# Attention steps taken in pairs, with the inserted projection tiles spread over the pairs, in a hybrid gMLP and differential-attention layer

## What is computed

```
h = rms_norm(x) * (1 + scale(c)) + shift(c)
u_a, v_a, z_a, q, k, v, z_b = split(h @ w_in)            # seven blocks of 512 columns
a_out = u_a * (tril(w_s) @ rms_norm(v_a) + b_s) * silu(z_a)       # chunks of 128 positions
q, k = rope(rms_norm(q)), rope(rms_norm(k))              # 8 half heads of 64
for each of 4 heads, causal:
    o = (softmax(q1 k1^T / 8) - lam * softmax(q2 k2^T / 8)) @ v     # v: 128 wide
b_out = rms_norm(o) * (1 - lam_init) * silu(z_b)
x = x + gate(c) * (concat(a_out, b_out) @ w_out)
```

## Time and profile before

| | |
|---|---|
| time, median of 3 runs | 527.22 us (526.07, 529.1, 527.22) |
| the profiled execution's own time | 524.75 us |
| its span, slowest core (core 0) | 523.7 us |
| spans of the eight cores | 518.9 to 523.7 us |
| mean granted TensorE clock by core | 0.969 to 0.977 |
| TensorE busy | 443.3 us (85% of the span) |
| VectorE busy | 334.4 us (64%) |
| ScalarE busy | 299.6 us (57%) |
| attention loop | about 273 to 489 us |
| after the last step | 489 to 523.7 us |

### The profile page before, as it was taken

How to read it: one execution, slowest core, us unless ns; L and a number is a source line. 1 busy time by engine, 2 the same in 40 slices (tenths; PEclk the granted TensorE clock), 3 DMA queues, 4 the chain that set the end, 5 groups by cost and what they waited for, 6 DMA issues and landing times.

```text
span 523.7 us, 9735 instructions; the slowest of 8 cores (518.9 to 523.7 us)
## 1 busy us (share of the span) xinstructions
PE 443.3 (85%) x3104; PEld 213.6 (41%) x3104; DVE 334.4 (64%) x761; ACT 299.6 (57%) x402; POOL 85.0 (16%) x118
## 2 busy tenths in 40 slices
PE   0036697999999999999979999989997999999395
PEld 0002243444444443443326554444554555555242
DVE  1236845664765478888872676788658857868732
ACT  1056477446543247677777666666777778777100
POOL 1112500003760000000001111122222222122100
PEclk9998989999999999999988999999999999999979
DMA  8998989237433200050021212116822032011113
GB/s 200 269 304 233 253 295 132 65 58 164 102 139 103 81 1 2 1 76 6 1 80 41 63 61 77 46 42 206 279 83 82 27 98 80 13 70 41 41 69 133
DMA packets 15605, 53.90 MB, mean 103 GB/s; under 512 B 2242, under 2 KB 2626, under 8 KB 14660
## 3 DMA queue, kind: packets, MB, share of 16 engines
q1 hardware_dynamic: 13924, 45.36, 26.8%
q0 software_dynamic: 1152, 7.50, 9.1%
q10 hardware_dynamic: 480, 0.41, 0.3%
HBM read 50.29 MB, written 8.39 MB: 112 GB/s over the span
## 4 chain that ended last, share of the span: by engine, by line
PE 62%; DMA 10%; DVE 8%; ACT 7%; issue 6%; POOL 4%; SPq 0%; DVEq 0%; ACTq 0%; POOLq 0%
PE psum L648 14%; PE psum L470 13%; PE psum L1045 9%; PE psum L923 8%; DMA sb_WO<-w_adaT 5%; PE psum L893 5%; PE psum L1011 4%; ACT sb_cs L906 4%; DMA sb_kT<-xT 4%; POOL sb_cs L911 4%; PE psum L682 2%; DVE sb_F L980 2%; PE psum L669 1%; DVE sb_F L939 1%; PE psum L671 1%
## 5 line engine op out<-in xcount | busy, mean ns | idle before, releaser
L906 ACT ACTIVATE sb_cs<-psum,sb_small 128x1024 bf16<-128x1024 f32 x144 | 151.0, 1114 | 58.6 <-PE psum L893 58.6
L923 PE MATMUL psum<-sb_vB,sb_cs 128*128 128x129 bf16 x1088 | 88.2, 223 | 9.6 <-POOL sb_cs L911 6.1
L923 PEld LDWEIGHTS psum<-sb_vB,sb_cs 128*128 128x128 bf16 x1088 | 63.3, 99 | 39.8 <-issue 39.3
L911 POOL TENSOR_TENSOR sb_cs<-sb_cs,sb_constb 128x256 bf16<-128x256 bf16 x64 | 44.3, 695 | 216.4 <-ACT sb_cs L906 211.9
L470 PE MATMUL psum<-sb_W,sb_hT 128*128 128x512 bf16 x256 | 62.3, 404 | 15.5 <-ACT sb_hT L466 12.6
L893 PE MATMUL psum<-sb_qT,sb_kT 64*128 64x256 bf16 (+1 forms) x576 | 56.4, 272 | 6.5 <-ACT sb_cs L906 2.9
L648 PE MATMUL psum<-sb_hT,sb_W 128*128 128x512 bf16 x256 | 60.2, 378 | 0.0
L357 DVE SCALAR_TENSOR_TENSOR sb_F<-sb_WO,sb_F 128x1024 f32<-128x1024 f32 x24 | 30.2, 1258 | 30.5 <-DMA sb_WO<-w_adaT 22.0
L470 PEld LDWEIGHTS psum<-sb_W,sb_hT 128*128 128x128 bf16 x256 | 25.8, 102 | 51.5 <-issue 26.1
L436 PE MATMUL psum<-sb_vnA,sb_constb 128*128 128x512 bf16 x32 | 11.0, 471 | 32.5 <-ACT sb_vnA L429 32.5
L939 DVE COPY sb_F<-psum 128x258 f32<-128x258 f32 x64 | 24.2, 420 | 20.4 <-PE psum L923 20.3
(11 more groups left out here) (113 smaller groups left out, 543.2 us busy)
## 6 DMA issues: line engine op xcount, KB each, us to landing
sb_WO<-w_adaT SPq DMA_DIRECT2D x24, 512.0 KB, 7.6
sb_W<-w_in POOLq DMA_DIRECT2D x5, 1024.0 KB, 10.5
sb_W<-x SPq DMA_DIRECT2D x8, 512.0 KB, 4.9
sb_cs<-w_out SPq DMA_DIRECT2D x8, 512.0 KB, 3.5
sb_hT<-x SPq DMA_DIRECT2D x8, 512.0 KB, 12.2
out<-sb_hT SPq DMA_DIRECT2D x8, 512.0 KB, 2.8
out<-sb_W SPq DMA_DIRECT2D x6, 512.0 KB, 3.2
sb_qT<-xT SPq DMA_DIRECT2D x4, 512.0 KB, 22.7
```

Of the source, the lines that this page charges most:

```text
L906: act(lambda E: E.activation(out=et, in_=psum[:, X:X + 2, :], func=AF.Exp, bias=negM, scale=0.125), reads=[pb[X], pb[Y], b_lam], writes=[b ...
L911: pool(lambda E, em=em: E.tensor_tensor(out=em, in0=em, in1=tri_b.unsqueeze(1).broadcast_to([128, 2, 128]), op=ALU.mult), reads=[b_e[ei], ...
L923: pe(lambda E, u=u, j=j, c=c, i=i: E.matmul(psum[:, j, 256 * c:256 * c + 129], lhsT=et[:, c, QB * u + 128 * j:QB * u + 128 * (j + 1)], rhs ...
```

## The change

The loop over steps becomes a loop over 72 pairs of steps. A pair issues exp of both steps, QK of the next two, then 4 or 5 matmuls of inserted tiles in turn (`quota`), PV of the first step, PV of the second. If the first of the two steps ends a group, its PV and `group_end` stand ahead of the inserted matmuls, which then lie between the two PV. A tile may be cut across pairs; it is evacuated at the end of the pair in which it was finished. Transposes are not counted in the quota. Per pair one or two tasks are popped. Eight matmuls, those of the two gate tiles, are issued ahead of the first pair. After the loop, tiles may use banks 2 to 7. All tasks and the last `fin_head` are issued, then up to 40 matmuls of output tiles, and only then the transposes of the last block. The functions that make tiles return their matmuls as a list, with the evacuation, in place of issuing them; `uu_owner` is an assertion and issues nothing.

```diff
-            later(now[0] + (2 if now[0] < NS else 0), outs)
-        return post
+            if h1 == 4:
+                later(now[0] + (2 if now[0] < NS else 0), outs)
+        return [mm], post
...
-    FB = [2, 3]
+    FB = [[2, 3]]
...
-    def fill_one():
-        it = fillq.pop(0)
-        kind, run, wt = it[0:3]
-        bank = FB[fb_ctr[0] % 2]
+    def open_tile():
+        it = fillq.pop(0)
+        kind, run = it[0:2]
+        bank = FB[0][fb_ctr[0] % len(FB[0])]
         fb_ctr[0] += 1
-        posts.append(run(bank))
...
+        if any(b_ == bank for b_, _ in posts):
+            run_posts()
+        mms, post = run(bank)
+        cur.append((kind, mms, bank, post))
+
+    def fill(n):
+        while n > 0 and (cur or fillq):
+            if not cur:
+                open_tile()
+            kind, mms, bank, post = cur[0]
+            if kind == "tr":
+                n += 1
+            while mms and n > 0:
+                mms.pop(0)()
+                n -= 1
+            if not mms:
+                cur.pop()
+                posts.append((bank, post))
...
-    ets = {}
-    for gs in range(NS + 1):
-        now[0] = gs
-        if gs < NS:
-            ets[gs] = do_exp(gs)
-        if gs + 2 < NS:
-            do_qk(gs + 2)
-        last = False
-        if gs > 0:
-            do_pv(gs - 1, *ets.pop(gs - 1))
-            jq, h, kp, first, last = gsteps[gs - 1]
-            if last:
-                group_end(gs - 1, jq, h)
+    NP = NS // 2
+    quota = 0.0
+    fill(8)
+    for p in range(NP):
+        g0, g1 = 2 * p, 2 * p + 1
+        now[0] = g0
+        e0 = do_exp(g0)
+        e1 = do_exp(g1)
+        if p + 1 < NP:
+            do_qk(g0 + 2)
+            do_qk(g0 + 3)
+        quota += 4.5
+        n = int(quota)
+        quota -= n
+        ends = [gsteps[g][4] for g in (g0, g1)]
+        if not ends[0]:
+            fill(n)
+        do_pv(g0, *e0)
+        if ends[0]:
+            group_end(g0, *gsteps[g0][0:2])
+            fill(n)
+        do_pv(g1, *e1)
+        if ends[1]:
+            group_end(g1, *gsteps[g1][0:2])
         run_posts()
-        run_due(gs)
-        if not last or len(taskq) > 5:
-            if taskq:
-                taskq.pop(0)()
-        if lowq and gs >= 9 and (gs - 9) % 5 == 0:
+        run_due(g1)
+        one_task()
+        if not (ends[0] or ends[1]) or len(taskq) > 4:
+            one_task()
+        if lowq and p >= 4 and p % 3 == 0:
             lowq.pop(0)()
-        if fillq and fillq[0][0] in ("tr", "gb"):
-            fill_one()
-        if (last or (gs > 0 and jq >= 6 and kp == 3)) and fillq and len(posts) < 2:
-            fill_one()
+    now[0] = NS
+    FB[0] = [2, 3, 4, 5, 6, 7]
+    fb_ctr[0] = 2 if fb_ctr[0] % 2 == 0 else 3
+    assert not lowq
+    while taskq or due:
+        while taskq:
+            one_task()
+        if due:
+            run_due(10 ** 9)
+        if fillq and fillq[0][0] == "tr":
+            break
+    trs = [fillq.pop(0)]
+    assert trs[0][0] == "tr" and (not fillq or fillq[0][0] != "tr")
+    fill(8 * 5)
+    fillq.insert(0, trs[0])
     s = NS + 1
-    while due or fillq or posts or taskq:
+    while due or fillq or posts or taskq or cur:
         now[0] = s
         run_posts()
-        while taskq:
-            taskq.pop(0)()
-            run_due(s)
         run_due(s)
-        for k in range(2):
-            if len(posts) < 2 and fillq:
-                fill_one()
+        fill(16)
         s += 1
```

More of the change, by code:

```diff
@@ L936, in group_end @@
         b = bpar[jq]
+        if h == 0:
+            assert uu_owner.get(b) is None, (jq, h)
+            uu_owner[b] = jq
         O4 = psum[:, 0:2, :].rearrange("p j (c x) -> p j c x", c=2)
@@ L987, in transposes, with mm @@
         tp = psum[:, bank, :].bitcast(BF16).rearrange("p (j h x) -> p j h x", j=2, h=4)
[L988 to L991, removed]
         h0, h1 = hs[0], hs[-1] + 1
+        def mm():
+            for j in range(2):
+                for h in hs:
+                    pe(lambda E, j=j, h=h: E.transpose(tp[:, j, h, :], fin[f][:, j, 128 * h:128 * (h + 1)], ident_b),
+                       reads=[b_constb, b_fin[f]], writes=[pb[bank]])
         def post():
@@ L1009, in run, with mm @@
             cols = slice(512 * tb, 512 * (tb + 1))
-            for kc in range(KC):
-                pe(lambda E, kc=kc: E.matmul(
+            def mm(kc):
+                pe(lambda E: E.matmul(
                     PS(bank), lhsT=wsl[0][:, kc, 128 * c4:128 * (c4 + 1)], rhs=hT[:, kc, cols],
@@ L1017, in post @@
                     reads=[pb[bank], b_uz[tb]], writes=[b_uz[tb]])
-            return post
+            return [lambda kc=kc: mm(kc) for kc in range(KC)], post
         return run
@@ L1039, in out_tile, with mm @@
         cc = slice(512 * half, 512 * (half + 1))
-        for m in range(KC):
+        def mm(m):
             if m < 4:
@@ L1044, in out_tile @@
                 lhsT, rd = qT[:, m - 4, rows_], b_qTh[tt // 2][m - 4]
-            pe(lambda E, lhsT=lhsT, m=m: E.matmul(PS(bank), lhsT=lhsT, rhs=woutb[:, m, cc], start=(m == 0), stop=(m == KC - 1)),
+            pe(lambda E: E.matmul(PS(bank), lhsT=lhsT, rhs=woutb[:, m, cc], start=(m == 0), stop=(m == KC - 1)),
                reads=[rd, b_wo], writes=[pb[bank]])
@@ L1056, in post @@
                     x_load(k + NX - 2)
-        return post
+        return [lambda m=m: mm(m) for m in range(KC)], post
     fillq = []
@@ L1081, in run, with mm @@
         def run(bank):
-            for k4 in range(4):
+            def mm(k4):
                 kc = 4 * half + k4
-                pe(lambda E, kc=kc, k4=k4: E.matmul(
+                pe(lambda E: E.matmul(
                     PS(bank, 128 * k4, 128 * (k4 + 1)), lhsT=ones_f, rhs=stg[:, 128 * kc:128 * (kc + 1)],
@@ L1094, in post @@
                         lowq.append(lambda m=m: wo_task(m))
-            return post
+            return [lambda k4=k4: mm(k4) for k4 in range(4)], post
         return run
@@ L1104, in _build_body @@
     now = [0]
+    cur = []
     def run_posts():
-        for fn in posts:
+        for bank, fn in posts:
             fn()
@@ L1124, in _build_body, with one_task @@
     out_n = [0]
-    def fill_one():
+    def open_tile():
         it = fillq.pop(0)
-        kind, run, wt = it[0:3]
-        bank = FB[fb_ctr[0] % 2]
+        kind, run = it[0:2]
+        bank = FB[0][fb_ctr[0] % len(FB[0])]
         fb_ctr[0] += 1
-        posts.append(run(bank))
[L1132 to L1141, removed]
+        if any(b_ == bank for b_, _ in posts):
[15 more added lines that the diff above has]
+                posts.append((bank, post))
+                if kind == "u":
+                    u_left[0] -= 1
+                    if u_left[0] == 0:
+                        b_xr[2].inherit([b_w[0]])
+                        b_xr[3].inherit([b_w[0]])
+                        for i in range(4, NX):
+                            b_xr[i].inherit([x for tb in range(TB) for x in b_h[tb]])
+                        for k in range(2, NX):
+                            x_load(k)
+    def one_task():
+        if taskq:
+            taskq.pop(0)()
     x_load(0)
```

2 lines of the change are left out of this document (added).

## The result

The changed kernel took 541.11 us (median; 539.32 to 544.47, 4 runs) against 527.75 us for the kernel before (526.07 to 529.1, 4 runs): a ratio of 1.0251, 95% interval 1.0214 to 1.0289. It is slower by 2.5%, where 507.7 us was forecast. The profiled execution took 544.47 us, its slowest core (core 7) spans 543.3 us.

What follows compares the result with a forecast made beforehand. TensorE and ScalarE were taken to bound the loop in turns. Start 273.5, work 192.5 and waits 12.6 gave 478.6 us; the end's 25.6 made 504.2 of span, 507.7 as run median; 8 in 10 range 498 to 519.

Steps and rivals of the forecast that it cites:

- TensorE's own work: Changed loop: pairs 107.7 us, inserted tiles 68.0 and 7.0, transposes, gate tiles and the slow start, 192.5 us in sum.
- The 0.10 for a boundary at each pair: Inserted tiles in the loop: 0.10 us extra at each of 70 pairs, 7.0 us in all.
- The price of QK: Pairs in the loop: each QK of a step was priced at 0.28 us, read from 296.95 to 297.23.
- its alternative: Pairs in the loop: QK behind QK at 0.22 us, not 0.28; 4.3 us less over 72 pairs, sum 188.2.
- the fourth of the sum, the waits: TensorE's waits in the changed loop, on ScalarE, the mask and the copy: 12.6 us in all.
- (a) ScalarE: Exps within a pair: ScalarE just keeps up, 2.88 against 2.92 us; 0.05 us a pair, 3.6 us in all.
- (b) The mask: PV waiting for the mask in 14 pairs that end a group with their first step: 4.2 us, before 6.1.
- (c) The copy: Copy out of banks 0 and 1 at a group's end: 0.15 us a group, 4.8 us in all.
- VectorE's queue: Rival, group ends: copies behind an evacuation and squares; TensorE waits 0.96 us 32 times, 31 us; time 534, chance 0.05.
- The clock rival: Rival, loop: denser work lowers the granted clock; at 13/16 it costs 44 us more, time 552, chance 0.03.
- Only the end gains: Rival: the loop's saving returns as small waits, last PV stays at 489 us; time 518, chance 0.24.
- The end: After the last PV: 37 matmuls ahead of the transposes, fifth tile waiting for bank 2; 25.6 us against 34.6 before.

Runs made afterwards that it cites:

- lean_pairs: `three` with w_out prepared in every second pair, and without the two sums of squares per group on VectorE; 507.25 us, ratio 0.9642 to the kernel before.
- three: The changed kernel with logarithm and exp behind the next pair's exps, no tile opened in a bank awaiting evacuation, VectorE tasks kept back at group ends; 520.59 us.
- task_gate: The changed kernel, but a pair ending a group pops a VectorE task only if more than four are listed, other pairs pop two; 534.56 us.

## Why the prediction was wrong

**TensorE's own work was put some 8 us too high.** At full clock and without a wait, a pair takes 2.63 us with five inserted matmuls (284.40 to 287.03) and 2.42 with four (301.22 to 303.64), 2.53 on the mean; the prediction's prices give 2.64.

```profile
284.40 0.61 PE L893 MATMUL psum<-sb_qT,sb_kT 64*128 64x256 bf16 x8
284.94 1.25 PE L1021 MATMUL psum<-sb_hT,sb_W 128*128 128x512 bf16 x5
...
287.03 0.56 PE L893 MATMUL psum<-sb_qT,sb_kT 64*128 64x256 bf16 x8
287.52 1.04 PE L1021 MATMUL psum<-sb_hT,sb_W 128*128 128x512 bf16 x4
288.40 1.07 PE L923 MATMUL psum<-sb_vB,sb_cs 128*128 128x129 bf16 x16
...
301.22 0.61 PE L893 MATMUL psum<-sb_qT,sb_kT 64*128 64x256 bf16 x8
...
303.64 0.76 PE L893 MATMUL psum<-sb_qT,sb_kT 64*128 64x256 bf16 x8
```

The 0.10 for a boundary at each pair isn't there: four inserted matmuls take 0.88 us (287.52 to 288.40), and 4 x 0.216 is 0.86. In the row of the kernel before from which it was taken, QK stood behind the tile; now PV does. The price of QK was misread as well: the QK at 296.95 belongs to the last step of a group, and two of its four matmuls are 64x128 (the row prints the shape of the first alone), so that its 0.28 us isn't a whole one's. A whole one takes 0.32, from 302.60 to the PV behind it:

```profile
302.92 0.51 PE L923 MATMUL psum<-sb_vB,sb_cs 128*128 128x129 bf16 x6
```

Two whole ones in a row take 0.54 (284.40 to 284.94), where the prediction kept 0.56 and its alternative gave 0.50; the 0.49 at 287.03 holds a last step's again. The Trainium skill, "TensorEngine Tiling (Array Packing)", section Key Properties, has TensorE drain at a change of the tiling mode; by it QK behind QK costs 0.22, and with the whole QK's 0.32 that is 0.54: by that rule, the trace agrees. With 0.11 less for each of 72 pairs the sum is 184.6 us in place of 192.5. So it is in part luck that the 207.4 us of `lean_pairs` lie so near to 205: its work is less than the sum had it, and its waits are 18 us on the median core in place of 12.6.

**The step that failed is the fourth of the sum, the waits.** 12.6 us stood there. On core 7 the loop has 14.7 (QK behind the exps), 7.9 (copy), 6.5 (evacuations: 6.3 and 3.1, less 2.9 that lie in the end), 2.6 (mask), 1.9 (u tile on the qT copy), 1.4 (on w_out) and 1.1 (the first QK behind the last projection tile) us, 36 together. The lower clock that follows them was a term put at nothing: 7% of 242 us are 17, and the sum holds some 3.5 of it, for the start of the loop alone. 184.6 + 36 + 13.5 is 234, and 241 was measured on core 7. Most of the 7 us left should be waits too short for the list, such as those inside the QK at 289.40, which takes 0.80 us in place of 0.54; that is an estimate. The prediction had named its own sign of being wrong, a last PV after 486 us; it came at 517.4. The other, over 15 us on the copy, did not come.

- (a) ScalarE. That it "just keeps up" was right to a few tenths of a us a pair where nothing else stood in its queue. What was left out is what else stands there, the two operations of `block_norm`, which the new unit of the due times moved ahead of VectorE's squares. The prediction followed the matmuls past the queues, and not these.
- (b) The mask: 4.2 forecast in 14 waits, 2.6 measured in 8. Right in kind, and small.
- (c) The copy: 4.8 forecast, 7.9 measured. The cause given, VectorE being late, was right; that the unconditional `one_task` puts squares ahead of the copy was not read from the diff.
- Not in the list at all: three tiles in one pair on two banks, 6.5 us and the 1.9 on qT.
- That a stand of TensorE is paid again in the clock was used for the end and not for the loop.

**The rivals.** VectorE's queue, at 534 us, named the right engine and the wrong wait: no 0.96 us at each of 32 groups' ends came, but single waits of up to 3.7 us. The clock rival was wrong in its form: in the loop the clock fell to the 1.2 GHz level behind stands, not under dense work. "Only the end gains" was forecast at 518, and `tail_only2`, which has only the new end, takes 517.9; the change as it was made is not that, since its loop got worse.

**The end** was right in its steps. The fifth tile waits 2.86 us for bank 2 and starts at 526.98, 9.3 us behind the last PV (9.5 forecast); the transposes begin at 528.70, 11.0 behind it (11.2 forecast); and from the last PV to the end core 7 takes 25.6 us (25.6 forecast). That this fits to the tenth is luck: it includes 0.85 us for a slow stretch, which didn't follow the stand of 2.86 us, and six of the other cores take some 1.5 us less than core 7. The chain of waits of core 7 there, to be set beside the earlier trace rows:

```profile
526.98 1.90 PE psum L1056 x8
...
530.74 4.49 PE psum L1056 x20
...
535.87 0.69 DVE sb_W L1060
536.62 2.86 DMA out<-sb_W
539.57 0.69 DVE sb_W L1060
```

## What to carry to other kernels

When a loop's step changes its unit, list every delay and condition that counts in the old unit (due times, tasks per iteration, how many buffers may be open) and follow each operation past the queue of its engine: here a 0.3 us operation waiting ahead of the exps cost up to 3.7 us of the bounding engine each time, and a slow stretch of its clock besides. A loop near one engine's bound is summed as work plus a list of all waits that its order can create, and it is the list that decides. Work that needs nothing of the last chain, as the output tiles ahead of the last transposes, was worth about 7 us and left the loop as it was (215.9 us against 215.5). And a price is to be read from an instruction of full size: the row of a group's last step looks like any other until its shapes are asked for.

## What the runs showed of the hardware that was not expected

A stand of TensorE was followed by a stretch at the 1.2 GHz level at eight places of the changed loop: behind 1.35 us busy in 5, the clock of 343.5 to 347 us is 0.60 with 3.43 busy in 3.5. Not every stand was: that of 2.5 us ahead of the PV at 324.9 us on core 7 had none behind it. With the waits repaired (`three`) one or two such places were left.

Before the loop, the profiled execution of the changed kernel shows another level on cores 4 to 7. A window of core 7:

```profile
158.00:164.00 6.00, 6.00 (x27) 2.42 (x25) 2.76 (x6) 3.28 (x6) 0.00 (x0) 0.81 0.60 176
```

18 to 31 us of each of these four cores are at 0.81, all before 166 us, in a part of the program that the change doesn't touch, and neither the profiled execution of the kernel before nor that of `three` shows it. On core 7 it costs some 6 us, and none of that is in the loop or the end as measured above. Of the sixteen profiled executions one more shows it: in that of `task_gate` cores 6 and 7 alone are at 0.81, for some 150 us each and inside the loop, and their loops take 235.8 and 234.6 us, against 225.4 to 230.0 on the other six. The prediction said that the trace disagrees with the rule of "TensorE: Matmul & The Clock Gate" (the Trainium skill, section "Seeing it yourself", where the rule stands) on such a level. The traces show that the level exists on this chip. That dense work on all cores always brings it they don't show: from 240 to 265 us all eight cores of the kernel before are at 1.00, and in `task_gate` two cores of a die were at 0.81 and the other two were not. What brings it, and whether denser work in the loop has a part in it, no run here shows.
